# Feed-forward of a two-layer transformer step: weight-block sums moved from GpSimd to VectorE, one row factor moved to the residual, another order within a unit

## The reference

```
def rms_norm(x, g):
    y = xf * lax.rsqrt(jnp.mean(xf * xf, axis=-1, keepdims=True) + EPS)
    return (y * g).astype(x.dtype)

def swiglu(h, w_gate_up, w_down):
    gu = h @ w_gate_up
    g, u = gu[..., :D_FF], gu[..., D_FF:]
    return (jax.nn.silu(g) * u) @ w_down

x = x + swiglu(rms_norm(x, norm_ffn_g[i]), w_gate_up[i], w_down[i])
```

## Time and profile before

| | |
|---|---|
| median of 3 runs | 1784.37 us |
| the profiled execution | 1783.48 us |
| its span in the trace | 1781.7 us |
| TensorE matmul busy | 1681.9 us, 94% |
| VectorE busy | 1163.0 us, 65% |
| ScalarE busy | 749.7 us, 42% |
| GpSimd busy | 510.0 us, 29% |
| TensorE's granted clock, mean | 0.996 |

### The profile page before, as it was taken

The page is one execution under the profiler, slowest core; times in us unless marked ns, Lnnn a source line. Parts: engine busy times, 40 slices in busy tenths (PEclk is TensorE's granted clock), DMA queues, the critical chain, the costliest instruction groups (busy, mean ns, idle before and its releaser), DMA issues.

```text
span 1781.7 us, 33276 instructions
## 1 busy us (share of the span) xinstructions
PE 1681.9 (94%) x14036; PEld 1549.3 (87%) x14036; DVE 1163.0 (65%) x1409; ACT 749.7 (42%) x1271; POOL 510.0 (29%) x325
## 2 busy tenths in 40 slices
PE   7999899999889999999999998999899999999998
PEld 7999666689889999999999995666899999999998
DVE  6663366667994598378632327777689946983883
ACT  5443355565442244134342206666455423441431
POOL 0000100004772386056000000000057714850660
PEclk9999999999999999999999999999999999999999
DMA  5125799921222122212223339998112221222222
GB/s 187 69 98 214 285 382 380 379 107 48 93 74 95 48 95 72 95 49 94 95 95 130 130 120 369 377 369 341 63 56 72 87 101 50 72 96 71 71 96 83
DMA packets 38463, 258.74 MB, mean 145 GB/s; under 512 B 4528, under 2 KB 4656, under 8 KB 9264
## 3 DMA queue, kind: packets, MB, share of 16 engines
q1 hardware_dynamic: 34560, 245.15, 37.1%
q0 software_dynamic: 3760, 11.54, 1.9%
HBM read 242.51 MB, written 13.11 MB: 143 GB/s over the span
## 4 chain that ended last, share of the span: by engine, by line
PE 61%; DVE 14%; POOL 11%; issue 9%; ACT 4%; DMA 0%; ACTq 0%; SPq 0%; DVEq 0%
PE ps L545 28%; PE ps L730 6%; POOL t L842 5%; DVE s_lo L700 4%; PE ps L257 4%; PE ps L258 4%; PE ps L259 4%; POOL t L844 3%; PE ps L1219 3%; POOL sg L858 2%; PE ps L1170 2%; PE ps L1123 2%; PE ps L581 2%; DVE up L944 2%; PE ps L1139 1%
## 5 line engine op out<-in xcount | busy, mean ns | idle before, releaser
L700 DVE TENSOR_TENSOR s_lo<-t,s_hi 128x512 fp32r<-128x512 f32 x176 | 207.2, 1188 | 16.8 <-ACT s_hi L696 16.5
L257 PE MATMUL ps<-w_hi,h_hi 128*128 128x256 f32 x640 | 183.1, 286 | 11.5 <-DVE h_lo L289 10.4
L235 DVE TENSOR_TENSOR w_lo<-w_raw,w_hi 128x2048 fp32r<-128x2048 f32 x55 | 126.0, 2291 | 98.9 <-ACT w_hi L227 89.1
L700 DVE TENSOR_TENSOR s_lo<-w_raw,s_hi 128x512 fp32r<-128x512 f32 x132 | 183.7, 1392 | 1.1 <-ACT s_hi L696 1.1
L258 PE MATMUL ps<-w_lo,h_hi 128*128 128x256 f32 x640 | 182.0, 284 | 0.0
L259 PE MATMUL ps<-w_hi,h_lo 128*128 128x256 f32 x640 | 182.0, 284 | 0.0
L227 ACT ACTIVATE w_hi<-w_raw 128x2048 fp32r<-128x2048 f32 x55 | 105.0, 1909 | 162.9 <-PE ps L545 154.5
L611 DVE TENSOR_TENSOR xT<-ps,xT 128x640 f32<-128x640 f32 x64 | 52.7, 823 | 180.4 <-PE ps L545 169.7
L696 ACT ACTIVATE s_hi<-t 128x512 fp32r<-128x512 f32 x176 | 108.6, 621 | 139.2 <-PE ps L730 68.1
L545 PE MATMUL ps<-gu_hi,w_hi 128*128 128x320 f32 x704 | 161.0, 310 | 6.2 <-issue 4.4
L730 PE MATMUL ps<-hs_hi,s_hi 128*128 128x320 f32 x528 | 163.6, 310 | 0.0
(11 more groups left out here) (244 smaller groups left out, 4303.2 us busy)
## 6 DMA issues: line engine op xcount, KB each, us to landing
w_raw<-in_w SPq DMA_DIRECT2D x99, 1024.0 KB, 4.8
kv<-in_k_s SPq DMA_DIRECT2D x30, 1024.0 KB, 7.9
kv<-in_v_a SPq DMA_DIRECT2D x18, 1024.0 KB, 8.0
work<-in_v_s SPq DMA_DIRECT2D x16, 1024.0 KB, 8.2
kv<-in_k_a SPq DMA_DIRECT2D x14, 1024.0 KB, 8.3
work<-in_v_a SPq DMA_DIRECT2D x14, 1024.0 KB, 8.6
extra<-in_k_a SPq DMA_DIRECT2D x8, 1024.0 KB, 7.2
w_raw<-in_k_a SPq DMA_DIRECT2D x8, 1024.0 KB, 8.7
```

The lines of the kernel that those rows point to most:

```text
L235: nc.vector.tensor_tensor(w_lo[s][:, :, :], w_raw[:, s, :, :], w_hi[s][:, :, :].bitcast(F32), ALU.subtract).then_inc(lo_done, 1)
L257: nc.tensor.matmul(out, s_hi, m_hi, start=first, stop=False, skip_group_check=True)
L700: nc.vector.tensor_tensor(s_lo[i][:, :, :], factor(j % 2, i), s_hi[i][:, :, :].bitcast(F32), ALU.subtract)\
```

## The change

Three things change, all in the feed-forward.

1. The sums of weight blocks leave GpSimd. `factor13` (a 128x1024 and a 128x512 difference) and `factor4` (128x512) become `sums12` and `sum4` on VectorE, with the same operands and the same counts of the semaphore `t`.
2. GpSimd's `scale` goes. `product` waits for silu alone, and `residual_dve` gets a chain argument `ch`: for the down tiles it multiplies the PSUM tile by `rstd_row` into `sg`, waits for that, and adds the result to `xT`.
3. The order in a unit changes: on VectorE `product` and `split_gu` of the unit before stand earlier, on ScalarE `split_gu` stands ahead of `copy_p5`.

GpSimd keeps `difference`, `add`, `gate_half` and `up_half`.

```
-        def residual_dve(dve, ph, after, hook):
+        def residual_dve(dve, ph, after, hook, ch=None):
...
-                    x = xT[:, 2 * j + n, :].rearrange("p (h c) -> p h c", h=2)
-                    nc.vector.tensor_tensor(x, banks(OUT[n]), x, ALU.add).then_inc(x_done, 1)
+                    x, y = halves(xT[:, 2 * j + n, :]), banks(OUT[n])
+                    if ch is not None:
+                        ch.link(nc.vector.tensor_tensor(halves(sg[:, n, :]), y, halves(rstd_row), ALU.mult))
+                        y = halves(sg[:, n, :])
+                    nc.vector.tensor_tensor(x, y, x, ALU.add).then_inc(x_done, 1)
...
+        def sums12(dve, g, j):
+            v = gu_at(g, j)
+            raw_ready(dve, g, j, j % 2)
+            if v > 0:
+                dve.wait_ge(lo_done, gu_split(v - 1, 4))
+            out, b0 = t13[:, :, :, :].rearrange("p a k c -> p (a k c)"), w_raw[:, j % 2, :, :]\
+                .rearrange("p k c -> p (k c)")
+            nc.vector.tensor_tensor(out, b0[:, 512:1536], b0[:, 0:1024], ALU.subtract).then_inc(ff["t"], 1)
+            dve.wait_ge(ff["t"], 3 * v + 1)
+            nc.vector.tensor_tensor(t2[:, :, :], raw_block(j % 2, 2), t13[:, 0], ALU.subtract).then_inc(ff["t"], 1)
+
+        def sum4(dve, g, j):
+            v = gu_at(g, j)
+            if j > 0:
+                dve.wait_ge(lo_done, split_count(g, j - 1, 6))
+            else:
+                dve.wait_ge(mm, tiles_before(unit_before(g), 4))
+            dve.wait_ge(ff["t"], 3 * v + 2)
+            nc.vector.tensor_tensor(t4[:, :, :], raw_block(j % 2, 3), t2[:, :, :], ALU.subtract).then_inc(ff["t"], 1)
+
         def first_los(dve, g, blocks):
+            sums12(dve, g, 0)
             for i in blocks:
                 gu_lo_block(dve, g, 0, i)
...
@@ ffn_act @@
+                    if j > 0:
+                        split_gu(v + j - 1, j - 1)
                     copy_p5(v + j, s)
                     if more:
-                        gu_hi_block(act, g, j + 1, 2)
-                        gu_hi_block(act, g, j + 1, 3)
+                        for i in range(2, 7):
+                            gu_hi_block(act, g, j + 1, i)
...
@@ ffn_pool @@
-            def factor13(g, j, v):
...
-            def factor4(g, j, v):
...
-            def scale(v, s):
-                pool.wait_ge(ff["silu"], v + 1)
-                nc.gpsimd.tensor_tensor(sg[:, s, :], sg[:, s, :], rstd_row, ALU.mult).then_inc(ff["sr"], 1)
...
@@ ffn_dve @@
                 if c == 0:
                     u2(v, 0)
+                sum4(dve, g, 0)
                 gu_lo_block(dve, g, 0, 5)
                 gu_lo_block(dve, g, 0, 6)
+                sums12(dve, g, 1)
+                sum4(dve, g, 1)
...
                     u2(v + j, s)
+                    if j > 0:
+                        product(v + j - 1, 1 - s)
                     if more:
                         gu_lo_block(dve, g, j + 1, 1)
+                    if j > 0:
+                        split_gu(v + j - 1, j - 1)
+                    if more:
                         gu_lo_block(dve, g, j + 1, 2)
-                    if j > 0:
-                        product(v + j - 1, 1 - s)
                     g0(v + j, s)
...
-                    if j > 0:
-                        split_gu(v + j - 1, j - 1)
+                    if j + 2 < n:
+                        sums12(dve, g, j + 2)
                     c12(v + j, s)
...
+                    if j + 2 < n:
+                        sum4(dve, g, j + 2)
                 dve.wait_ge(ff["c21"], v + n)
...
-                dve.wait_ge(ff["silu"], v + n)
-                nc.vector.tensor_tensor(sg[:, 1, :], sg[:, 1, :], rstd_row, ALU.mult).then_inc(ff["sr"], 1)
                 product(v + n - 1, 1)
```

More of the change, by code:

```diff
@@ L600, in residual_act, with halves @@
                 hook(act, j)
-        def residual_dve(dve, ph, after, hook):
+        def halves(x):
+            return x.rearrange("p (h c) -> p h c", h=2)
+        def residual_dve(dve, ph, after, hook, ch=None):
             for j in range(4):
@@ L642, in pair_dve @@
             return lambda dve, j, n: norm.odd_dve(dve, j) if n else norm.even_dve(dve, j)
-        ff = sems("ff", "t p1 p5 u2 u3 g0 c12 c21 c22 g1 silu sr gu hi lo")
+        ff = sems("ff", "t p1 p5 u2 u3 g0 c12 c21 c22 g1 silu gu hi lo")
         prod = sem("prod")
@@ L869, in up_half @@
                     .then_inc(ff["c22"], 1)
-            for p in range(2):
+            for p in range(4):
                 nm.difference(pool, p)
@@ L874, in ffn_pool @@
                 nm.add(pool, 2 * p + 1)
-            nm.difference(pool, 2)
             for c, n, g, d, v in chunks(f):
-                factor13(g, 0, v)
-                if c == 0:
-                    nm.add(pool, 4)
-                    nm.add(pool, 5)
-                    nm.difference(pool, 3)
-                    nm.add(pool, 6)
-                factor4(g, 0, v)
-                if c == 0:
-                    nm.add(pool, 7)
-                factor13(g, 1, v + 1)
                 for j in range(n):
@@ L889, in ffn_pool @@
                         pool.wait_ge(*nm.rooted)
-                    s = j % 2
                     if j > 0:
-                        gate_half(v + j - 1, 1 - s)
-                    if j + 1 < n:
-                        factor4(g, j + 1, v + j + 1)
-                    if j > 0:
-                        scale(v + j - 1, 1 - s)
-                    up_half(v + j, s)
-                    if j + 2 < n:
-                        factor13(g, j + 2, v + j + 2)
+                        gate_half(v + j - 1, 1 - j % 2)
+                    up_half(v + j, j % 2)
         def gu_split(v, i):
@@ L907, in gu_split, with ffn_dve @@
                 r -= n
-        def ffn_dve(dve, f, nm, hook):
+        def ffn_dve(dve, ch, f, nm, hook):
             def u2(v, s):
@@ L940, in product @@
             def product(v, s):
-                dve.wait_ge(ff["sr"], v + 1)
+                dve.wait_ge(ff["silu"], v + 1)
                 dve.wait_ge(ff["c12"], v + 1)
@@ L972, in ffn_dve @@
                         gu_lo_block(dve, g, 1, 6)
+                        sums12(dve, g, 2)
+                        sum4(dve, g, 2)
                         continue
@@ L1005, in ffn_dve @@
                 if c + 1 < len(CHUNKS):
-                    residual_dve(dve, d, lambda e: first_los(e, f"g{f}{c + 1}", range(4)), nothing)
+                    residual_dve(dve, d, lambda e: first_los(e, f"g{f}{c + 1}", range(4)), nothing, ch)
                 else:
-                    residual_dve(dve, d, lambda e: split_lo(e, d, 4, 0), hook)
+                    residual_dve(dve, d, lambda e: split_lo(e, d, 4, 0), hook, ch)
         def flat(x):
@@ L1918, in _ @@
             residual_dve(dve, "oa", lambda e: first_los(e, "g00", range(4)), pair_dve(norms["ffn0"]))
-            ffn_dve(dve, 0, norms["ffn0"], whole_dve(norms["kv"]))
+            ffn_dve(dve, ch, 0, norms["ffn0"], whole_dve(norms["kv"]))
             dve.wait_ge(norm["rstd"], 2)
@@ L1931, in _ @@
             residual_dve(dve, "ob", lambda e: first_los(e, "g10", range(4)), pair_dve(norms["ffn1"]))
-            ffn_dve(dve, 1, norms["ffn1"], nothing)
+            ffn_dve(dve, ch, 1, norms["ffn1"], nothing)
         @block.tensor
```

21 lines of the change are left out of this document (removed).

## The result

The changed kernel takes 1737.59 us (median of 4 runs, 1736.54 to 1737.93), the kernel before 1785.26 us on the same chip (4 runs, 1782.86 to 1787.31). The ratio is 0.973 with a 95% interval of 0.972 to 0.975: 2.7% faster. 1739 was forecast. The profiled execution of the changed kernel took 1736.5 us with a span of 1734.8, that of before had a span of 1781.7; the difference to account for is 46.9 us.

What follows compares the result with a forecast made beforehand. VectorE, held by GpSimd over shared SBUF ports, makes TensorE lose 1.37 us per steady unit. The terms sum to 45.0 us, 1739.4 against the median; forecast 1739, range of 8 in 10 1730 to 1764.

Steps and rivals of the forecast that it cites:

- steady units: 26 units in the middle of chunks: each loses 1.37 us to VectorE, which goes; gain 35.6 us.
- units 1 and starts of chunks 2 and 3: Second and third chunks: units 1 gain 2.0 us at `u3`; the first `u2` comes 0.4 later, costing 1.6.
- ends of chunks: Six down phases start without waiting for a late `split_gu`, 0.95 us each; gain 5.7 us.
- starts of layers, the wait for the lo block: Product 6 at two layer starts: TensorE idle 2.1 us there plus 0.4 before it; gain 0.7 us each.
- starts of layers, behind that wait: Low granted clock after the wait costs 1.2 to 1.7 us; half taken as gained, 0.7 us per layer.
- `gu_lo` in the third chunks: Two third chunks: the down phase's 0.90 us wait for the last `gu_lo` shrinks by 0.7 each; gain 1.4 us.
- end of the kernel: Behind the last down tile the added multiply makes the final add 0.86 us later: -0.9 us.
- the list of 12.0 to 12.1: VectorE's time per steady unit in us, bounds 10.7 and 13.3, narrowly under TensorE's 12.31.
- The two collisions: Steady unit: `up_half` holds VectorE's fourth block or `sums12`, `gate_half` its last block or `sum4`; 0.73 us each, 1.46 together.
- The first rival: VectorE still bounds steady units with a list longer than 12.31 us: 1755, or 1765 at the upper bound; chance 0.18.
- the third: Rival: lo blocks keep 1.39 us for another reason, period about 16, 60 us slower, 1840; chance 0.05.
- the second rival: A late `product`, now ahead of five operations, holds VectorE's queue and delays `u3`: near 1780 us; chance 0.05.

Runs made afterwards that it cites:

- the added read: Changed kernel plus a useless 128x512 GpSimd addition of two SBUF operands behind `up_half` in most units: 1753.5 us, ratio 0.983 to the kernel before.
- the added writes: Changed kernel plus three GpSimd memsets of 128x640 in a row behind `up_half` in most units: 1738.0 us, ratio 0.974 to the kernel before.
- the first experiment: Kernel before with only the new order of ScalarE and VectorE; sums and `scale` stay on GpSimd: 1809.2 us, ratio 1.014.
- The experiment that moved the sums: Changed kernel with unit 1's `sums12` and `sum4` behind `u2` and `u3` of unit 0 in the second and third chunks: 1737.4 us, ratio 0.974.
- The run with one write: Changed kernel plus one GpSimd memset of 128x640 behind `up_half` in most units: 1737.0 us, ratio 0.974 to the kernel before.
- The last two experiments: Changed kernel with unit 1's sums behind `u2` and `u3` in later chunks: 1737.4 us; the same with `up_half` and `gate_half` on VectorE too: 1735.8 us.

## Why the prediction was right, step by step

The terms of the sum, in us. Measured is worked out from the phases above and the waits in both traces; the steady term is 26 x (13.68 - 12.33).

| step | forecast | measured |
|---|---|---|
| steady units | 35.6 | 35.1 |
| units 1 and starts of chunks 2 and 3 (2.0 - 1.6) | 0.4 | 0.2 |
| ends of chunks | 5.7 | 5.3 |
| starts of layers, the wait for the lo block | 1.4 | 1.5 |
| starts of layers, behind that wait | 1.4 | 2.8 |
| `gu_lo` in the third chunks | 1.4 | 1.6 |
| end of the kernel | -0.9 | -0.8 |
| not forecast | | 1.2 |
| sum | 45.0 | 46.9 |

**Exclusion, and the list of 12.0 to 12.1.** Right: the list is 11.91, with 0.28 of it a wait for `split_gu`'s hi part. The two collisions came at the operations named (fourth block or `sums12`; `sum4`). They cost 0.61 and 0.57 in a steady unit, and 0.49 in place of the 0.61 where `sums12` is the one held; 0.73 was allowed for each. That the total came out so near is partly luck. The forecast list is 10.3 of VectorE's own work, 0.4 of waits and 1.46 of holds; the measured one is 10.6, 0.28 and 1.06. The own work was put too low because `sums12` and `sum4` each wait for the block before them: they start 0.10 and 0.04 behind its end (501.55, 505.54), where 0.08 ahead of it was reckoned. The rule of the Trainium skill ("SBUF — State Buffer", section "Who interferes with whom"), that a VectorE instruction with two SBUF inputs contends with a GpSimd instruction that reads SBUF and not with one that only writes, agrees with the added read (1.67 for 0.69) and with the added writes (1.23 for 1.23). The estimate of 11.3 for mere sharing did not come.

**TensorE sets the unit.** Right: 12.33 against 12.31, with no wait for `u3` in any steady unit. The first rival (12.6 or more) did not come, and the third (blocks slow for another reason) is excluded by 691 ns in 132 blocks.

**The order.** Right in its place and size: 0.89 x 6 for 0.95 x 6. What the prediction did not say is that the order alone costs 25 us. It gave the second rival 0.05 with the argument that `gate_half` no longer stands behind a sum of 3 us; the first experiment, in which GpSimd keeps its sums and `scale`, shows how much hung on that. The prediction timed the second path, by `copy_p5` on ScalarE behind `split_gu` (ready 6.9, due 8.7), but didn't count it to this rival; in the first experiment it is the larger of the two waits.

**Starts of chunks.** `u2` was forecast 0.4 later than before, and is 0.5 later (1.08 for 0.58). The terms as the prediction lists them, with five lo blocks, give 613.95 and not its 613.4; with the four that stand ahead of `u2` in the list they give 613.3, 7.5 behind the chunk's first matmul, and 7.7 was measured. The experiment that moved the sums expected too much; VectorE has the same work there wherever the sums stand.

**Starts of layers.** The term that was mis-sized, 2.8 for 4.3, and not by the wait: that was forecast at 2.1 and is 2.09 in one layer and 2.45 in the other. Behind it the prediction took 0.7 per layer for a clock that might not fall, and 1.4 and 1.3 came back. Before, product 6 of unit 1 came 15.08 us after that of unit 0 (450.92 to 466.00): 12.31 is work, 1.16 the wait for `u3` in front of it, and 1.6 the low clock. Now it is 13.64 (450.31 to 463.95), at a granted clock of 1.00, with 0.30 and 0.80 of waits. That looks like the clock's doing, but is so in small part only. The run with three writes has the same wait in the first layer, 2.09 before product 6 at 451.08, and there the clock did fall. The stretch that matches the window above:

```profile
452.77:456.27 3.50, 3.50 (x17) 3.50 (x16) 3.50 (x7) 0.63 (x2) 0.87 (x1) 0.58 0.00 0
```

While TensorE is slow VectorE catches up, both waits are gone, and the step is 13.92 (451.08 to 465.00). So the level of the clock is worth 0.3 of the 1.4 there. In the other layer it is worth less still: the step is 13.82 at the full level, and 13.84 in the run that moved the sums, where the clock fell. The rest is the wait of 1.16 for `u3` in unit 1 of each layer's first chunk, a term that the prediction left out: it counted units 1 of the other chunks alone.

That the clock stayed up in the profiled execution is luck besides. Over the changed kernel and the runs that have its sums on VectorE, waits of 2.09 to 2.46 us at this place were followed by the low level in 4 of 16 cases, and waits of 3.0 us, in the kernel before and the other two, in 5 of 6. Taking half was a fair guess at the clock, and the prediction came near with a term missing.

**Not forecast.** 1.2 us between the two layers' feed-forwards: from 850.04 to 1319.91 it was 469.87, from 827.46 to 1295.36 it is 467.90, and 0.8 of the difference is the `gu_lo` counted above. Most or all of the rest lies in a stretch at the low clock that the profiled execution of before has and that of the changed kernel hasn't: its granted clock is 0.72 from 1260 to 1266, and 1.00 in the changed kernel from 1236 to 1242. The run with one write, which is as fast as the changed kernel, has 0.72 there too, so such a stretch belongs to the single execution and not to the change.

**The expectations of the experiments.** The sums alone were expected at 1760 to 1772 and came at 1746.5: the hold by `scale` was overestimated, since I placed a PSUM operation outside it that runs within. The bounds in the prediction used the same charge, so its upper bound of 13.3 for the list was too cautious. The order alone was expected at about 1820 with a period of 15.1 and came at 1809 with 14.5. The factor alone and the old order came just below their ranges (1747.2 for 1748 to 1762, 1742.7 for 1743 to 1745). The last two experiments were expected too low, 1733 to 1735 and 1730 to 1734 for 1737.4 and 1735.8: what was moved out of one wait mostly came back in the next.

## What to carry to other kernels

Where VectorE and GpSimd both work out of SBUF, the busy time of VectorE isn't its work: take the free duration of each operation from a row beside an idle GpSimd, and count a hold as about the GpSimd instruction's length less what VectorE does meanwhile from PSUM. Moving work onto the engine that is late can make it faster, here by 9.8 us of 99 with 23 more instructions, if that work was holding it from the other engine. When several parts of a change relieve the same bound, each alone may bring most of the gain, and a reordering can be harmful without them; measure it with and without.
